# A fused transformer kernel on one core: 96 instead of 64 tokens by gathered expert rows, 416-wide dense matmuls, rounding moved to ScalarE, a smaller first attention block

## The reference

```
sc = einsum('chkd,cd->chk', u_tab[idx], xc)       # idx: 8 heads x 16 chosen experts per token
a = gelu(sc);  g = softmax(scores of the chosen)
out = einsum('chk,chkd->cd', g * a, v_tab[idx])
```

## Time and profile before

| | us |
|---|---|
| median of 3 runs (2937.28 to 2939.71) | 2938.76 |
| the profiled execution | 2947.47 |
| its span, first to last instruction | 2945.6 |

### The profile page before, as it was taken

One profiled execution on the slowest core, in us unless ns is written; L12 is line 12 of the kernel. 1 busy time (PEld: TensorE's weight loads), 2 busy tenths in 40 slices (PEclk: granted clock), 3 DMA queues, 4 the chain that ended last, 5 costly groups with the idle time before them and its releaser, 6 DMA issues. The chain is left out here.

```text
span 2945.6 us, 47942 instructions
## 1 busy us (share of the span) xinstructions
PE 2756.6 (94%) x18360; PEld 2381.0 (81%) x18360; DVE 1722.3 (58%) x2972; ACT 1041.7 (35%) x1631; POOL 815.4 (28%) x560
## 2 busy tenths in 40 slices
PE   6999989999999999999999999799699878999996
PEld 4766778989999999889999999667499775888775
DVE  1354359976888886267777777546566644333115
ACT  3366333443333333312222222354244444333223
POOL 2622333454111110000111110133354232444442
PEclk9999999999999999999999999899899989999998
DMA  3211222446777776667777777323832101322231
GB/s 119 87 58 52 85 93 81 136 145 181 252 260 281 272 257 221 223 235 251 250 251 258 257 257 243 112 94 96 276 78 47 28 8 59 98 97 96 100 100 65
DMA packets 191900, 453.63 MB, mean 154 GB/s; under 512 B 57360, under 2 KB 106640, under 8 KB 190480
## 3 DMA queue, kind: packets, MB, share of 16 engines
q1 hardware_dynamic: 173328, 384.56, 39.9%
q0 software_dynamic: 18432, 67.12, 6.9%
HBM read 376.12 MB, written 75.50 MB: 153 GB/s over the span
## 5 line engine op out<-in xcount | busy, mean ns | idle before, releaser
L152 ACT ACTIVATE weights_high<-weights_raw 128x1024 fp32r<-128x1024 f32 x433 | 458.7, 1059 | 1491.1 <-PE psum L260 1431.7
L160 POOL TENSOR_TENSOR weights_low<-weights_raw,weights_high 128x1024 fp32r<-128x1024 f32 x219 | 537.9, 2456 | 854.7 <-ACT weights_high L152 854.7
L258 PE MATMUL psum<-expert_in_high,weights_high 128*128 128x448 f32 (+1 forms) x1152 | 434.7, 377 | 6.2 <-DVE expert_in_low L353 4.3
L260 PE MATMUL psum<-expert_in_high,weights_low 128*128 128x448 f32 (+1 forms) x1152 | 425.9, 370 | 0.0
L259 PE MATMUL psum<-expert_in_low,weights_high 128*128 128x448 f32 (+1 forms) x1152 | 425.6, 369 | 0.0
L258 PE MATMUL psum<-coefficients_high,weights_high 128*128 128x448 f32 x1024 | 379.7, 371 | 4.5 <-DVE coefficients_low L1252 4.5
L259 PE MATMUL psum<-coefficients_low,weights_high 128*128 128x448 f32 x1024 | 378.6, 370 | 0.0
L260 PE MATMUL psum<-coefficients_high,weights_low 128*128 128x448 f32 x1024 | 378.4, 370 | 0.0
L160 DVE TENSOR_TENSOR weights_low<-weights_raw,weights_high 128x1024 fp32r<-128x1024 f32 x214 | 261.3, 1221 | 142.5 <-ACT weights_high L152 133.6
L258 PEld LDWEIGHTS psum<-expert_in_high,weights_high 128*128 128x128 f32 x1152 | 217.6, 189 | 29.3 <-issue 5.1
L1342 POOL DMA_INDIRECT expert_rows<-in_weights,row_numbers x64 | 60.0, 938 | 649.7 <-DVE s_by_token_then_row_sums L1378 489.4
(11 more groups left out here) (401 smaller groups left out, 5071.0 us busy)
## 6 DMA issues: line engine op xcount, KB each, us to landing
weights_raw<-in_weights SPq DMA_DIRECT2D x435, 512.0 KB
expert_activations<-expert_activation SPq DMA_DIRECT2D x128, 224.0 KB
coefficient_table<-table_stage SPq DMA_DIRECT2D x8, 3584.0 KB, 14.0
table_group<-coefficient_table SPq DMA_DIRECT2D x128, 224.0 KB, 4.4
activation_in<-expert_activations SPq DMA_DIRECT2D x128, 224.0 KB, 3.9
chunk_b_k_v<-scan_vectors SPq DMA_DIRECT2D x8, 768.0 KB, 5.8
scan_vectors<-scan_stage SPq DMA_DIRECT2D x4, 1280.0 KB, 6.9
scan_vectors<-scan_stage SPq DMA_DIRECT2D x4, 1024.0 KB, 6.3
```

Source lines behind the costliest of these rows:

```text
L152: act.activation(d.hi[:, m % SPLIT, :], d.raw[:, m % RAW, :], ACT.Copy).then_inc(d.high, 1)
L160: pool.tensor_tensor(d.lo[:, m % SPLIT, :], d.raw[:, m % RAW, :], d.hi[:, m % SPLIT, :].bitcast(F32), ALU.subtract).then_inc(d.split, 1)
L258: pe.matmul(acc, w[0][:, cols], x[0], start=start, stop=False)
L260: return pe.matmul(acc, w[1][:, cols], x[0], start=False, stop=stop)
```

## The change

It has five parts. (1) `GT` goes from 64 to 96: the dense tokens are 416 in eight blocks of 52, the tokens by rows 96. Rows come in two groups: 64 gathers with two choices for each of tokens 0 to 63, and 32 gathers with four choices for each of tokens 64 to 95 (quarters of the partitions), so 96 gathers of U and 96 of V. (2) Dots: one in every one of the 72 table slots, and two in each of the first 12 end slots; GELU of the dots moves from end slot 1 to 14. Adds: 96 over 120 tiles. (3) The table loop is written as 2 x 36 slots with four blocks each (the blocks stay at nine slots, now 13 steps). (4) In the V half DVE makes the product once, in place, one tile ahead; ACT rounds it (`rounded`), after the `high` of the same tile; DVE subtracts. (5) Attention's first eight steps compute, scale, transpose and multiply their own 128 keys alone; two memsets on POOL go.

```diff
-GT = 64
+GT = 96
 TD = T - GT
-TB = 56
+TB = 52
 NTB = TD // TB
...
@@ attention @@
+        def blocks(n):
+            return range(0 if n >= QC else 1, 2)
+
+        def seen(n):
+            return slice(blocks(n)[0] * P, 2 * P)
...
-                        mm = pe.matmul(ps[:, score_bank(n) + half, 0:2 * P], q[rows(half), c, block_of(n)],
-                                       keys[rows(half), n // QC * P:n // QC * P + 2 * P], start=True, stop=True)
+                        mm = pe.matmul(ps[:, score_bank(n) + half, seen(n)], q[rows(half), c, block_of(n)],
+                                       keys[rows(half), (n // QC + blocks(n)[0]) * P:(n // QC + 2) * P], start=True, stop=True)
...
-                        for kb in range(2):
+                        for kb in blocks(n):
...
@@ Experts @@
-    TBL, TBS = 4, 18
+    TBL, TBS, BLK = 2, 36, 4
...
@@ experts, scalar @@
-                    if j == 1:
+                    if j == ex.END - 2:
                         rows.activate(act)
                 w.advance(ex.END)
-                w.run(act, w.high, ex.ut // 16 - 1, 16)
+
+                def rounded(ii, j):
+                    o = j % ex.CR
+                    act.wait_ge(ex.part, ii * 16 + (j + 1))
+                    act.wait_ge(dense.used, ii * 16 + (w.slots + j + 1 - ex.CR))
+                    act.activation(co[0][:, o, :], a_in[:, j % ex.AR, :], ACT.Copy).then_inc(ex.high, 1)
+
+                for j in range(ex.CR):
+                    rounded(0, j)
+                with act.Fori(0, ex.ut // 16 - 1) as ii:
+                    for j in range(16):
+                        w.high(act, ii, j, 16)
+                        rounded(ii, j + ex.CR)
...
@@ experts, vector @@
-                            if j < rows.N:
-                                rows.dot(dve, j)
+                            rows.dot(dve, j)
                 w.advance(ex.TBL * ex.TBS)
+                dots = ex.TBL * ex.TBS
                 for j in range(ex.END):
                     w.low(dve, 0, j, ex.END)
+                    for s in range(dots + 2 * j, min(dots + 2 * j + 2, rows.N)):
+                        rows.dot(dve, s)
                     if j == ex.END - 1:
                         rows.weigh(dve)
...
-                    dve.wait_ge(dense.used, w.slots + n + 1 - ex.CR)
-                    tile, gt = a_in[:, r, :], g[:, par, :, j % GI8, :]
-                    dve.tensor_tensor(by_block(co[0][:, o, :]), by_block(tile), gt, ALU.mult).then_inc(ex.part, 1)
-                    dve.tensor_tensor(by_block(tile), by_block(tile), gt, ALU.mult).then_inc(ex.part, 1)
-                    dve.wait_ge(ex.part, 2 * n + 2)
-                    dve.tensor_tensor(co[1][:, o, :], tile, co[0][:, o, :].bitcast(F32), ALU.subtract).then_inc(ex.coef, 1)
+                    dve.tensor_tensor(by_block(a_in[:, r, :]), by_block(a_in[:, r, :]), g[:, par, :, j % GI8, :],
+                                      ALU.mult).then_inc(ex.part, 1)
+
+                multiply(0)
+                for n in range(ex.ut):
+                    if n + 1 < ex.ut:
+                        multiply(n + 1)
+                    o = n % ex.CR
+                    dve.wait_ge(ex.high, n + 1)
+                    dve.tensor_tensor(co[1][:, o, :], a_in[:, n % ex.AR, :], co[0][:, o, :].bitcast(F32),
+                                      ALU.subtract).then_inc(ex.coef, 1)
                     if n >= SPLIT:
                         w.low(dve, 0, n - SPLIT, ex.ut)
                     rows.add_rows(dve, n, ex.ut)
...
@@ Rows @@
-    R, N = 4, P // 2
-    HALVES = (slice(0, GT), slice(GT, 2 * GT))
+    R = 4
+    GROUPS = ((0, 64), (64, 32))
+    N = sum(width for _, width in GROUPS)
...
     def turn_inputs(self, pe):
...
+        for g, (first, width) in enumerate(self.GROUPS):
+            for half in range(2):
+                n = 2 * g + half
+                if n == 3:
+                    pe.wait_ge(self.copied, 1)
+                for c in range(4 * half, 4 * half + 4):
+                    for part in range(2):
+                        tokens = self.xn[part][:, c, first:first + width].bitcast(F32)
+                        for p in range(0, P, width):
+                            mm = pe.matmul(self.k.ps[p:p + width, self.bank(n), c % 4 * P:(c % 4 + 1) * P], tokens,
+                                           self.k.consts("ident"), start=part == 0, stop=part == 1)
                 mm.then_inc(self.turned, 1)
...
-        pe.matmul(self.k.ps[:, c, 0:GT], self.x[:, c * P:(c + 1) * P], self.k.consts("eye2"), start=False, stop=False)
+        for g, (first, width) in enumerate(self.GROUPS):
+            pe.matmul(self.k.ps[:, c, first:first + width], self.x[:, g, c * P:(c + 1) * P], self.same_token(g),
+                      start=False, stop=False)
```

More of the change, by code:

```diff
@@ L906, in exp @@
                         j, head = 2 * n + half, n % QC * 2 + half
-                        act.activation(e[:, n % 2, half, :], s[:, n % 2, half, :], ACT.Exp, bias=nm[:, j:j + 1],
+                        act.activation(e[:, n % 2, half, seen(n)], s[:, n % 2, half, seen(n)], ACT.Exp, bias=nm[:, j:j + 1],
                                        accum_out=su[:, j:j + 1]).then_inc(exps, 1)
@@ L925, in _ @@
                     act.wait_ge(turned, n + 1)
-                    act.activation(pt[:, :], ps[:, TURNED, :], ACT.Copy).then_inc(copied, 1)
+                    by_half = (x.rearrange("p (h n) -> p h n", h=2)[:, :, seen(n)] for x in (pt[:, :], ps[:, TURNED, :]))
+                    act.activation(*by_half, ACT.Copy).then_inc(copied, 1)
                     if n + 2 < STEPS:
@@ L956, in __init__ @@
         self.g_in = [sem(f"table_group_loaded{n}") for n in range(2)]
-        self.part, self.coef, self.summed, self.added = (sem(n) for n in (
-            "coefficient_parts", "coefficients_ready", "expert_sums_ready", "expert_sums_added"))
+        self.part, self.high, self.coef, self.summed, self.added = (sem(n) for n in (
+            "coefficients_multiplied", "coefficients_rounded", "coefficients_ready", "expert_sums_ready", "expert_sums_added"))
     def steps_after(self, q):
-        n = self.TBS // 2
+        n = self.TBS // self.BLK
         return range(q * self.STEPS // n, (q + 1) * self.STEPS // n)
@@ L1094, in _ @@
                 with pe.Fori(0, ex.TBL) as i:
[L1095 to L1097 removed]
+                    for par in range(ex.BLK):
+                        for q in range(BLOCK_S):
+                            j = par * BLOCK_S + q
                             up(i, ex.TBS, TABLE0 + j, j)
@@ L1129, in _ @@
                 for c in range(DC):
-                    rows.add_halves(pe, c)
+                    rows.add_parts(pe, c)
                     for j in range(16 - SPLIT, 16):
@@ L1180, in _ @@
                     up(0, 0, END0 + j, j)
-                    if j == 1:
+                    if j == ex.END - 2:
                         rows.activate(act)
                 w.advance(ex.END)
-                w.run(act, w.high, ex.ut // 16 - 1, 16)
+                def rounded(ii, j):
[9 more added lines that the diff above has]
+                        rounded(ii, j + ex.CR)
+                w.advance(ex.ut - 16)
+                end = ex.ut // 16 - 1
                 for j in range(16 - SPLIT):
                     w.high(act, 0, j, 16)
+                    act.wait_ge(ex.part, end * 16 + (j + ex.CR + 1))
+                    act.wait_ge(dense.used, w.slots + j + 1)
+                    act.activation(co[0][:, j % ex.CR, :], a_in[:, (j + ex.CR) % ex.AR, :], ACT.Copy).then_inc(ex.high, 1)
                 norm.preload(act)
@@ L1293, in __init__, with group, same_token @@
         self.loaded = [k.semaphore(f"row_loaded{r}") for r in range(self.R)]
+    def group(self, s):
+        return next(g for g, (first, width) in enumerate(self.GROUPS) if s < first + width)
+    def same_token(self, g):
+        return self.k.consts(("eye2", "eye4")[g])
     def turn_inputs(self, pe):
-        for c in range(DC):
-            for r in self.HALVES:
-                for part in range(2):
-                    mm = pe.matmul(self.k.ps[r, 2 + c // 4, c % 4 * P:(c % 4 + 1) * P], self.xn[part][:, c, 0:GT].bitcast(F32),
-                                   self.k.consts("ident"), start=part == 0, stop=part == 1)
-            if c % 4 == 3:
+        for g, (first, width) in enumerate(self.GROUPS):
[9 more added lines that the diff above has]
+                                           self.k.consts("ident"), start=part == 0, stop=part == 1)
@@ L1311, in turn_choices @@
     def turn_choices(self, pe):
-        pe.wait_ge(self.copied, 1)
+        pe.wait_ge(self.copied, 4)
         for j in range(3):
-            for r in self.HALVES:
-                mm = pe.matmul(self.k.ps[r, 2, j * self.N:(j + 1) * self.N], self.sel[r, j, 0:GT], self.k.consts("eye2")[r, :],
-                               start=True, stop=True)
+            for g, (first, width) in enumerate(self.GROUPS):
+                for p in range(0, P, width):
```

(4 more changed lines are left out.)

81 lines of the change are left out of this document (41 added, 40 removed).

## The result

The changed kernel takes 3125.21 us (median of 4 runs, 3118.23 to 3130.42); the kernel before, run beside it, 2939.24 (4 runs). The ratio is 1.0624, 95% interval 1.0599 to 1.0649. 2855 was forecast. The profiled execution took 3118.23 us, its span is 3116.4.

The account below looks back on a forecast made before the run. PE, busy for 94% of the span, was taken to bound the kernel. The terms sum to −83.7 us, mostly dense matmuls (−81.9): 2947.5 to 2863.8 for the profiled execution, 2855 from the median of 2938.8; range 2816 to 2900.

Parts of the forecast that it names:

- the paragraph on the V half: V half's coefficient chain per tile: 3.6 us of 4.64, slack 1.0 us, so no cost; last tile's chain +0.2 us.
- My note on transfers in that half: V half's transfers: 1.37 MB a tile, 295 GB/s against 251 before; cost 0, end +6 us.
- The rivals: Four alternatives: matmul gap not following the columns (10%), DMA as bound (4%), V chain too long (5%), better than thought (4%).
- a chain in V that is too long: V half: ScalarE late by 0.3 us beyond the slack on each tile, 38 us in all, 2893 us; chance 5%.
- The DMA rival: From slot 40 on, DMA is the bound at a steady 268 GB/s: +121 us, 2973 us; chance 4%.
- The dense matmuls: U slots and V tiles: 448 to 416 columns saves 13.3 ns on each of 6144 matmuls, −81.9 us.
- The end stage: U half's slots 112 to 127: row transfers just fit at 418 GB/s, late rows cost +3 us, ends 0 and +18.
- The table stage: U half's slots 40 to 111: a slot every 5.84 us, table steps 104 instead of 112 (−7.1 us), no VectorE wait.
- the rewritten loop of part 3: Table stage: a block still takes nine slots, so the stages and the wait for a stored block keep their places.
- Inputs turned: On PE between ranking and slot 0: turning the inputs for two row groups, +4.3 us; choices turned, +0.5 us.
- All that follows V's last low part: After V: two small matmuls instead of one for each of 8 chunks, +1.8 us; last tile's chain, +0.2 us.
- my range: 2816 to 2900 us: matmul price (−29, +20), end stage at +15, tiles at +6, inputs at +2.7.

Follow-up runs that it names:

- Mended and spread: Changed kernel with product in turn or old products, end-stage loads spread over slots: 2865.53 and 2866.63 us; the former with one V-loop turn written out, 2861.99.
- the last column of the table: Stage times of the changed kernel with the product in turn and end-stage loads spread: 2865.53 us, V half 574.3 us over 127 tiles.
- the mended kernels: Changed kernel with reload before weight load (2887.31 us), product in its own turn (2873.55), old products (2877.69) or eight activation_in buffers (2879.91), and later kernels built on these.
- the spread kernel: Changed kernel with product in turn, table_group loads one in each of slots 4 to 11, activation_in reloads one in each of the last four: 2865.53 us.
- longer program: Kernel before with one of seven V-loop turns written out, PE's program 384 matmuls longer: 2936.91 us, ratio 1.0001.

## Why the prediction was wrong

**The step that failed** stands in the paragraph on the V half: "The product for n is made one tile ahead (its ScalarE reader is 5 us off), the adds follow the low part. Slack 1.0 us: 0." I followed the moved product forward, to its reader, and not back, to what it waits for. The chain that I summed, high, rounding, subtraction, low, began at "tile n−2 used" and took the data in `activation_in` as there. My note on transfers in that half was about bandwidth alone (295 GB/s). The rows for the right sum were in the trace of before, the timeline of SyncE and VectorE:

```profile
1502.85 0.33 SPq L1045 DMA_DIRECT2D activation_in<-expert_activations  x1
...
1504.09 0.62 DVE L1249 TENSOR_TENSOR coefficients_high<-activation_in,table_group 128x448 fp32r<-128x448 f32 x1 [0.80 <-PE psum L260]
...
1509.05 0.63 DVE L1249 TENSOR_TENSOR coefficients_high<-activation_in,table_group 128x448 fp32r<-128x448 f32 x1 [2.00 <-PE psum L260]
```

The reload of 1502.85 is for the product of 1509.05; with 3.9 us to land, the median of these loads in that kernel, 2.3 us are left. One turn earlier the product would stand at 1504.1, 2.7 us before the data. And since the product stands on VectorE ahead of the low part that frees SyncE, that lateness is not paid once but closes a loop. It cost 1.95 us a tile, 248 us in 127 tiles (823.8 against 575.6).

The Trainium skill has the rule that I passed over (DMA: Bandwidth & Descriptors, Anatomy of one DMA — SWDGE (gpsimd) path): "any semaphore wait happens on the issuing sequencer before dispatch". The section is on GpSimd's transfers; SyncE's behave so in the trace of the changed kernel: `activation_in` is issued 0.57 and 0.53 us behind `weights_raw` in the two turns from 1501 us, although its own buffer had been free since a subtraction two turns before.

**The rivals.** None was this one. The nearest gave 5% to a chain in V that is too long "because VectorE's adds (1.28 each) or the reload of weights push it", at 0.3 us a tile; its sign, PE waiting for `coefficients_low` once a tile, did not show (PE waited for `weights_low`). The DMA rival had half of its signature, PE waiting for the low part, and the right side. The other half did not show: ScalarE's rounding of the weights waited for PE (601 us from 1260 to 2040), not for `weights_raw`. Its mechanism is refuted: the share fell to 0.59, and seven kernels with the same bytes run at 2862 to 2887 us. Its price, 2973, was not the measured one either.

**The dense matmuls**, −81.9 us: right, and the level of 193.3 ns in V too high. The columns' 13.3 ns are what the width costs; slots 0 to 40 took 190.0 us where 189.7 were forecast. In V the gain was 18 ns, of which 4.0 come from the slow pattern of the profiled execution of before; by the inference above its median does not have them. The Trainium skill's figures (TensorE: Matmul & The Clock Gate, Back-to-back issue gap; about 81 ns at 128 columns, 131 at 512) make 0.13 ns a column by my estimate; between 384 and 432 the rows show 0.47.

**The end stage**, +3 us with ends 0 and +18: mis-sized, and for the wrong reason. It cost 17 us over PE's own 68.2 (84.9; 84.6 to 86.2 in the others with four buffers), near the upper end. I had divided bytes by a rate; what made 8 to 12 of the 17 us was that the 12 loads stand in one slot of a queue that the weights use as well, while the gathers fill the engines. Spread, 4.6 to 8.6 us are left.

**The table stage**, −30.1 us with its matmuls: 450.5 became 424.8 to 428.1, forecast 420.4. The difference is one event. In all eight kernels with the loop of 2 x 36 slots, slot 76, the first of the loop's second turn, takes 10.2 to 13.3 us, where the slots nine before and nine behind it take 6.35; in the six kernels with 4 x 18 it takes 6.65 like those. PE waits there for nothing that the profile shows, 2.1 us in the changed kernel (up to 4.3 in the others), and its granted clock is 0.63 in the 4.6 us behind it:

```profile
920.37 0.46 PE L258 MATMUL psum<-expert_in_high,weights_high 128*128 128x416 f32 x1 [2.07 <-issue]
```

This is a second term that I had put at nothing, the rewritten loop of part 3: where it begins its second turn 3.9 to 6.9 us are lost; the rest of the stage is within 1 us of the forecast. No kernel has part 3 without the 96 rows, so that the loop is the reason is not shown, and what PE waits for is open.

**Inputs turned** and ranking: records of 7.1 us for 3.5, +3.6 where I took +4.3. **The handover behind V**: not in my sum, VectorE's wait is 5.3 us longer in all kernels with 96 rows, cause open. All that follows V's last low part takes 2.4 to 6.7 us more than before, of which +2.0 was forecast.

Mended and spread, the kernel takes 2862 to 2867 us. My 2855 was 7 to 12 too low for that. That it came so near is in part luck: in the last column of the table I had 7.5 us too little in the table stage, 4.7 behind V and 3.5 elsewhere, and 14.8 too much in V, most of it the slow pattern of the profiled execution. The bounds of my range also don't follow from the terms named beside them, which make about 2822 and 2896, not 2816 and 2900.

## What to carry to other kernels

When work is moved earlier, price it at both ends: who reads it, and what releases what it reads. For a transfer that is the place of its issue in the queue, with every wait ahead of it in the same queue, plus its time to land; if what stands ahead waits for something behind the moved work, the lateness recurs in every turn. A ring of buffers helps only as far as the issue runs ahead of the use, so count the turns between them, and ask the same of every burst of loads that shares a queue with a stream that the bound engine lives on.

## What the runs showed of the hardware that I had not expected

- With 448 columns the same stream of matmuls runs in one of two patterns, 206.7 or 202.7 ns a matmul, for hundreds of us, and changes between them within one execution: 13 us over a V half. 416 wide showed 188.4 to 188.8 ns on the mean of the V half in the mended kernels in which PE does not wait there.
- Issuing gets dear in a burst: one load of `table_group` a slot took SyncE 0.37 to 0.48 us in the spread kernel; eight in a row took 4.68 us and the four `activation_in` behind them 4.41, 1.1 us each. The DMA share was about 1.00 in both, so full engines alone don't make the difference.
- VectorE's wait at the handover behind the V half is 12.5 us in each of the kernels with 96 rows, whatever else they have, and 7.2 in each of those with 64, part 4 or longer program or not.
- PE stands 2.1 to 4.3 us where the loop of 36 slots begins its second turn, in each of the eight kernels that have it, and nowhere in the table stage behind slot 40 in the kernels with loops of 18 slots.
